# Two decoder blocks in one kernel: ACT builds the compressed blocks, the last gates move beside the embedding, the rotation angles follow the norm

## The reference, cut to what matters

```python
# first block, layer i
def compress(kv, pe, w1, w2):            # 31 overlapping blocks of 32 tokens, stride 16
    blocks = kv[:, :, idx, :] + pe       # pe: position inside the block
    return jax.nn.silu(blocks.reshape(B, G, NC, 32 * dh) @ w1) @ w2
...
h = h + concatenate([y_hg, y_nsa]) @ w_out[i]
gate = jax.nn.sigmoid(rmsnorm(h, ple_norm_g[i]) @ w_pg[i])
h = h + gate * (p[i] @ w_pp[i])          # p[i] @ w_pp[i]: the embedding
...
# second block, layer 0
x = layer_norm(a * x + 0.5 * swiglu_ffn(x, ...))
h = diff_attention(x, ..., cos(positions * inv), sin(positions * inv), ...)
```

## Time and profile before

| | us |
|---|---|
| Three timed runs: median (lowest to highest) | 3279.15 (3272.29 to 3296.4) |
| The profiled execution: its own time | 3269.5 |
| Its span, first to last instruction | 3267.7 |
| PE busy | 3063.7 (94%) |
| POOL, DVE, ACT busy | 1363.3, 1165.8, 1100.6 |
| Granted clock of PE, mean over the span | 0.968 |

### The profile page before, as it was taken

The page is one execution under the profiler, slowest core; times in us unless marked ns, Lnnn a source line. Parts: engine busy times, 40 slices in busy tenths (PEclk is TensorE's granted clock), DMA queues, the critical chain, the costliest instruction groups (busy, mean ns, idle before and its releaser), DMA issues.

```text
span 3267.7 us, 58661 instructions
## 1 busy us (share of the span) xinstructions
PE 3063.7 (94%) x24228; PEld 2806.5 (86%) x24228; DVE 1165.8 (36%) x1930; ACT 1100.6 (34%) x1823; POOL 1363.3 (42%) x656
## 2 busy tenths in 40 slices
PE   7999898999899999989889999999999978999998
PEld 7987488987578999979469789998999967789997
DVE  1535742444743111152751541103211085441103
ACT  4233633223633222131634342223222133432222
POOL 5533044443133454444026255444445444254543
PEclk9999999999999999999989999999999998999999
DMA  5211013212012223222013222232233231122231
GB/s 190 71 55 62 1 65 115 73 46 72 14 52 73 96 96 103 90 76 86 19 64 109 69 81 96 96 103 78 92 101 101 96 112 62 55 84 96 96 103 58
DMA packets 72202, 262.22 MB, mean 80 GB/s; under 512 B 8032, under 2 KB 8672, under 8 KB 70912
## 3 DMA queue, kind: packets, MB, share of 16 engines
q1 hardware_dynamic: 69728, 249.77, 23.2%
q10 hardware_dynamic: 2336, 10.49, 0.9%
HBM read 258.13 MB, written 2.10 MB: 80 GB/s over the span
## 4 chain that ended last, share of the span: by engine, by line
PE 81%; DVE 11%; issue 4%; ACT 2%; POOL 2%; DMA 0%; POOLq 0%; ACTq 0%; DVEq 0%
PE bank L527 24%; PE bank L509 15%; PE bank L511 15%; PE bank L513 15%; PE bank L668 1%; PE bank L841 1%; PE bank L873 1%; PE bank L857 1%; POOL wl L381 1%; PE bank L1080 1%; DVE small L2086 1%; DVE s L1673 1%; PE bank L719 1%; PE bank L1071 1%; DVE h L1968 1%
## 5 line engine op out<-in xcount | busy, mean ns | idle before, releaser
L381 POOL TENSOR_TENSOR wl<-raw,wh 128x1024 fp32r<-128x1024 f32 x464 | 1154.2, 2502 | 1815.8 <-ACT wh L1147 1815.6
L1147 ACT CAST wh<-raw 128x1024 fp32r<-128x1024 f32 x464 | 472.1, 1047 | 1053.9 <-PE bank L513 837.6
L509 PE MATMUL bank<-xh,wh 128*128 128x256 f32 x3168 | 641.1, 284 | 0.0
L511 PE MATMUL bank<-xl,wh 128*128 128x256 f32 x3168 | 625.1, 279 | 0.0
L513 PE MATMUL bank<-xh,wl 128*128 128x256 f32 x3168 | 624.5, 279 | 0.0
L509 PEld LDWEIGHTS bank<-xh,wh 128*128 128x128 f32 x3168 | 485.0, 190 | 19.7 <-issue 18.3
L513 PEld LDWEIGHTS bank<-xh,wl 128*128 128x128 f32 x3168 | 484.1, 190 | 0.0
L511 PEld LDWEIGHTS bank<-xl,wh 128*128 128x128 f32 x3168 | 484.0, 190 | 0.0
L527 PE MATMUL bank<-xh,wh 128*128 128x256 f32 x1952 | 392.5, 283 | 54.1 <-ACT xh L1199 36.6
L527 PE MATMUL bank<-xh,wl 128*128 128x256 f32 x1952 | 390.1, 282 | 0.0
L527 PEld LDWEIGHTS bank<-xh,wh 128*128 128x128 f32 x1952 | 304.2, 194 | 65.2 <-issue 64.5
(11 more groups left out here) (336 smaller groups left out, 3816.6 us busy)
## 6 DMA issues: line engine op xcount, KB each, us to landing
raw<-in_slabs SPq DMA_DIRECT2D x464, 512.0 KB, 3.3
h<-in_x_t SPq DMA_DIRECT2D x8, 256.0 KB, 5.3
w1v<-in_w ACTq DMA_DIRECT2D x2, 1024.0 KB, 4.7
side<-in_pp_w ACTq DMA_DIRECT2D x2, 1024.0 KB, 5.3
xm<-in_mem_t ACTq DMA_DIRECT2D x2, 1024.0 KB, 4.8
out<-h SPq DMA_DIRECT2D x8, 256.0 KB, 2.0
side<-in_w SPq DMA_DIRECT2D x1, 1024.0 KB, 12.6
vt<-in_p_t ACTq DMA_DIRECT2D x2, 512.0 KB, 6.2
```

Of the source, the lines that this page charges most:

```text
L381: nc.gpsimd.tensor_tensor(wl[:, n % RING, :], raw[:, n % RING, :], wh[:, n % RING, :], A.subtract).then_inc(w_low, 1)
L509: nc.tensor.matmul(dst[:, c], high_l, high_r[:, c], start=first and n == 0, stop=False)
L511: nc.tensor.matmul(dst[:, c], high_l, low_r[:, c], start=False, stop=False)
L1147: nc.scalar.copy(wh[:, slot, :], raw[:, slot, :]).then_inc(w_high, 1)
```

## The change

Three edits, which share no code:

1. *Compressed blocks.* `placed` moves from POOL to ACT. Where POOL made eight positions at once (two instructions of 128x496 for each tensor), ACT makes one position with each instruction, 16 of 128x62 for each tensor, as an Identity activation with the embedding's column as bias. ACT copies `kk_k` one chunk earlier.
2. *Last gates.* A new semaphore, `gates`, is raised when the fourth pair's product is done, ahead of its embedding; ACT's last sigmoids wait for it. DVE waits for the embedding itself. In layer 1, squares and sums of squares are left out (no norm reads them), `split` copies each chunk as soon as it is final, the two weight slabs that `pg` cast are cast inside `split` behind the sixth copy, and DVE makes six of the eight lower halves ahead of the last gates.
3. *Angles.* The three DMAs of `da_prep` are issued in the norm before it, between ACT's wait for the first statistic and the square of the mean. DVE goes on to `da_prep` when `h` is written, without waiting for POOL's `xl`. The clamp of `r` (input of the first sine) is put ahead of the two steps that make `r2`.

```diff
-    "front": dict(... kk=8, blocks=4, ...),
+    "front": dict(... kk=8, blocks=32, ...),
...
 # POOL, front
                     low(chunk0 + 11 + lv)
-                    if lv == 4:
-                        placed(0, kk_k, blocks_k)
-                    if lv == 5:
-                        placed(1, kk_v, blocks_v)
...
 # PE, hidden
-                        pe.wait_ge(S["blocks"], st["blocks"] + 2 * b + 2)
+                        pe.wait_ge(S["blocks"], st["blocks"] + 16 * b + 16)
...
 # PE, pg
                     last = pair(st["slab"] + 2 * j, j % 2, xh, xl, T, *two_steps)
+                    if j == 3:
+                        last.then_inc(S["gates"], 1)
...
 # ACT, norm
                 act.wait_ge(S["stat"], st["stat"] + 1)
+                if (st["kind"], st["layer"], st["which"]) == ("ln", 0, 0):
+                    act.dma_start(dpos[:], positions.broadcast_to([P, T])).then_inc(block2_in, 16)
+                    act.dma_start(dspr[:], spread).then_inc(block2_in, 16)
+                    act.dma_start(rot_m, rot2).then_inc(block2_in, 16)
...
 # ACT, split of layer 1
-                    act.wait_ge(S["r"], st["r"])
-                    split_of(st, lambda c: h[:, c, :])
+                    for c in range(KC):
+                        act.wait_ge(S["r"], st["r"] - KC + c + 1)
+                        nc.scalar.copy(xh[:, c, :], h[:, c, :]).then_inc(S["xh"], 1)
+                        if c == KC - 3:
+                            high(st["slab"] - 2 + RING)
+                            high(st["slab"] - 1 + RING)
...
 # ACT, front
+                def placed(b, kk, x):
+                    act.wait_ge(S["kk"], st["kk"] + 4 * b + 4)
+                    tok = kk.rearrange("p g (c i r) -> p i g c r", i=8, r=2)[:, :, :, :, 0]
+                    for i in range(16):
+                        nc.scalar.activation(x[:, i, :].rearrange("p (g c) -> p g c", g=2),
+                                             tok[:, i % 8, :, i // 8:i // 8 + NC], F.Identity,
+                                             bias=par(COL1, "pe", (st["layer"] * 2 + b) * 16 + i)).then_inc(S["blocks"], 1)
...
 # ACT, pg
+                    else:
+                        act.wait_ge(S["gates"], st["gates"] + 1)
...
 # DVE, norm
-                if unsplit:
+                if unsplit or (ln and (st["layer"], st["which"]) == (0, 0)):
                     dve.wait_ge(S["hn"], st["hn"] + KC)
...
 # DVE, pg
                     dve.wait_ge(took_a, st["took"] + j + 1)
+                    if j == 3:
+                        if st["layer"]:
+                            for c in range(KC - 2):
+                                lower(st, c, h[:, c, :])
+                        dve.wait_ge(prod, st["prod"] + 4)
...
 # DVE, da_prep
                 step(V.tensor_scalar(r2, r, float(np.pi / 2), None, A.add))
+                V.tensor_scalar(r, r, PI, -PI, A.min, A.max).then_inc(S["dp_v"], 1)
                 step(V.tensor_scalar(k, r2, float(np.pi), None, A.is_gt))
```

More of the change, by code:

```diff
@@ L84 @@
     "split": dict(xh=KC, xl=KC),
-    "front": dict(slab=36, prod=36, took=2, ev_a=ACT_TOOK[-1], ev_v=DVE_TOOK[-1], kk=8, blocks=4, cmp_p=5, cmp_a=5,
+    "front": dict(slab=36, prod=36, took=2, ev_a=ACT_TOOK[-1], ev_v=DVE_TOOK[-1], kk=8, blocks=32, cmp_p=5, cmp_a=5,
                   cmp_v=3, lvl_k=4 * (LEVELS - 2), lvl_v=4 * LEVELS, lvl_p=4 * LEVELS, lbs=2, ax=12, hpv=4, ob=4,
@@ L90 @@
     "w_out": dict(slab=8, prod=4, took=4, r=KC // 2, sq=KC // 2, s2=KC - 2, s1=1, e2=1),
-    "pg": dict(slab=8, prod=4, took=4, r=KC, sq=KC, s2=KC - 2),
+    "pg": dict(slab=8, prod=4, took=4, gates=1, r=KC, sq=KC, s2=KC - 2),
     "ffn_in": dict(slab=2 * NF, prod=NF, took=NF, hh=NF, hv=NF, hl=NF),
@@ L130, in plan @@
             add["xh"] = add["xl"] = KC
+        if kind == "pg" and layer == 1:
+            add["sq"] = add["s2"] = 0
         if kind == "w_out" and which == 0:
@@ L424, in decayed @@
                         nc.gpsimd.tensor_tensor(k, k, cat(odd, k.shape[2]), A.mult).then_inc(S["lvl_k"], 1)
[L426 to L434, removed]
                 def cosine(j):
@@ L1289, in head_out @@
                     nc.scalar.copy(ob[:, hd, :], bank[hd][:]).then_inc(S["ob"], 1)
-                for j in range(11):
+                for j in range(10):
                     chunk(j)
@@ L1294, in front @@
                 pairs_of(kk_k, proj[:, KCM, :])
+                chunk(10)
+                placed(0, kk_k, blocks_k)
                 chunk(11)
@@ L1297, in front @@
                 pairs_of(kk_v, proj[:, VCM, :])
-                for j in range(12, 14):
-                    chunk(j)
+                chunk(12)
+                placed(1, kk_v, blocks_v)
+                chunk(13)
                 table(F.Silu)
@@ L1463, in pg @@
                     nc.scalar.activation(sg[:, 1, :], bank[2 * (j % 2) + 1][:], F.Sigmoid).then_inc(took_a, 1)
-                    if j == 3:
-                        table(F.Abs_reciprocal_sqrt)
-                        high(st["slab"] + 2 * j + RING)
-                    squares(st, 2 * j)
-                    squares(st, 2 * j + 1)
-                high(st["slab"] + 7 + RING)
+                    if st["layer"] == 0:
+                        if j == 3:
+                            table(F.Abs_reciprocal_sqrt)
+                            high(st["slab"] + 2 * j + RING)
+                        squares(st, 2 * j)
+                        squares(st, 2 * j + 1)
                 if st["layer"] == 0:
+                    high(st["slab"] + 7 + RING)
                     act.dma_start(side[:], w1[1, 0]).then_inc(w1k_in, 16)
@@ L1736, in split @@
             def split(st):
-                for c in range(KC):
+                for c in range(KC - 2 if st["which"] == 1 else 0, KC):
                     lower(st, c, (proj[:, (HGO if c < 4 else NZ - 4) + c, :], h[:, c, :], xq[:, c, :])[st["which"]])
@@ L2014, in pg @@
                         V.tensor_tensor(h[:, c, :], h[:, c, :], tb[:, o, :], A.add).then_inc(S["r"], 1)
+                    if st["layer"]:
+                        dve.wait_ge(S["r"], st["r"] + 2 * j + 2)
+                        continue
                     for o in range(2):
```

10 lines of the change are left out of this document (4 added, 6 removed).

## The result

| | median | runs |
|---|---|---|
| before | 3282.0 us | 14 (3269.4 to 3310.4) |
| changed | 3259.8 us | 14 (3247.2 to 3277.2) |

The ratio is 0.994, with a 95% interval of 0.9919 to 0.9961: 20 us less (13 to 27; the medians differ by 22). It lies beside the forecast's 3263 and its -15.7 us. The profiled executions are only 10.1 us apart (span 3267.7 and 3257.6), less than the change's own places give; that difference is the first thing to explain.

What follows compares the result with a forecast made beforehand. PE was taken as the bound, 81% of the chain. Terms -15.1 - 0.25 + 0.1 - 0.45 = -15.7 us on the profiled 3269.5, carried in proportion to the median 3279.15, gave 3263 us; range 3251 to 3279.

Steps and rivals of the forecast that it cites:

- Term A: Front, recurrence steps of both layers: moving the blocks' positions off POOL removes most of four PE waits; -15.1 us, bounds -16 and -6.
- Rival 1: Front: POOL's `hk` multiplies follow `wl` and hold DVE instead; 8.4 us stay, gain 8.3, about 3271 us; chance 12%.
- Nothing for ACT: Front: both sets of 16 activations fit into ACT's idle time, so no cost was taken for ACT.
- 16 are 3.5 us: Front, ACT: one set of 16 activations, sized from a 0.22 us activation of the same width, takes 3.5 us.
- activations of `blocks` at about 0.2 us: Front, ACT: sign that the forecast is right, each activation for the positions lasting about 0.2 us.
- the cover ends at (9.1 - 1.6) / 16 = 0.47 us each: Front, ACT: values' activations stay hidden up to 0.47 us each, since `hidden()` reads them 9.1 us after the product.
- Rival 3: `hidden()`, both layers: PE waits for ACT's second set; 3285 us in all at 1.05 us per activation; chance 3%.
- Term B0: Layer 0's last gates: sigmoids start earlier, but POOL's `wl` holds DVE's adds; -0.25 us, bounds 0 and -1.3.
- Term B1: Layer 1's last gates and split: POOL's `wl` holds DVE's sixth lower half; +0.1 us, bounds +0.5 and -1.9.
- Rival 4: Layer 1's last gates: gates early, but PE starts no earlier because `took_v` is late; inside the forecast, no separate chance.
- Term C: Rotation angles: operand earlier by 1.0 and 0.15, less 0.7 for the DMA issues; -0.45 us, bounds +0.7 and -4.5.
- So I take no gain: First rotation, L975: PE might keep its clock after a shorter wait of about 2.5 us; counted as 0.

## Why the prediction was right, step by step

- **Term A, -15.1: right, -15.2 measured** in the windows, -15.6 in the sections, -15.1 between whole kernels. The residue taken from the level before was right too (0.15 to 0.2 us for each place; the step of 2.40). Rival 1's mechanism is real and its price was too high: POOL's `hk` follows `wl` at once and holds DVE's second multiply, but only for 0.48 us of 0.66, and PE doesn't stand. The working has two slips that move nothing: the four stands are 10.2 us, not 10.4, and by its own figures rival 1 gains 16.4 - 8.4 = 8.0 us, not 8.3.
- **Nothing for ACT: right in the sum, wrong in two of its steps.** "16 are 3.5 us" was mis-sized, and so was the sign "activations of `blocks` at about 0.2 us": 4.80, a third more. Of the 1.3 us too little, 0.9 is the stride (3.90 from consecutive words) and 0.4 is there without it. And "the cover ends at (9.1 - 1.6) / 16 = 0.47 us each" came near the measured 0.50 for the wrong reason: it looked at who reads the blocks, while the first to suffer is POOL's `hk`, queued behind a `wl` that waits for ACT's cast. Rival 3 was real, its place was not, and its price was too low: at 0.73 us each its formula gives 16 x 0.73 - 7.5 + 1.6 = 5.8 us a layer, the run paid 10.
- **Term B0, -0.25: the hold was right** (2.18 us for the two adds), the start came 0.34 earlier. The further 0.8 us of the two executions shown is not the change's. From the embedding's first matmul (3464) to number 3564 it is 28.8, 27.2 and 27.2 us in three executions with the old gates, 26.9 in four with the new ones and 28.4 in the run with consecutive words, without the slower pace: 0.34 less, and 1.6 more when the clock falls otherwise.
- **Term B1, +0.1: the mechanism was right** to 0.02 us (POOL first by 0.15, forecast 0.13; the sixth half held), the size was short: "L2009 and L2010 end at 1030.57, and PE starts at 1030.7" left 0.1 us for what took 0.55 (L2025's end at 1019.25 to PE's start at 1019.80). +0.47 in seven executions with six halves ahead. Two hundred matmuls behind the embedding's start (6936 to 7136) nothing of it can be seen: 34.0 to 34.6 us in three executions with the old order, 33.8 to 34.8 in the seven. Rival 4, that PE does not start earlier for `took_v`, describes it.
- **Term C, -0.45: the DMA issues right** (+0.7, measured 0.73, and gone when moved); the cast's end earlier by 1.4, with those 0.7 taken out, instead of 1.0. From the second statistic to a point behind the first rotations (matmuls 10120 to 10300), without the slower pace, 37.4, 35.7 and 35.7 us in three executions with the old code and 35.4, 35.2, 35.2 and 33.4 in four with the new: -1.5 on average, with up to 2.0 between executions of one code. "So I take no gain" for the clock was the step that was too careful, and the before trace's wait of 3.65 was the longer one of 3.65, 3.0 and 3.0 in three executions with the old code.
- **Sum**: -15.7 forecast, -17.8 by places in the two executions shown (-17 with B0 at -0.34), -15 between whole kernels without the slower pace, -20 (13 to 27) timed. Carrying the profiled difference over to the median was sound, but the prediction took the runs' scatter, 7 us, as mere noise around one time. In the profiled executions most of it is the slower pace, in steps of 14 us; that this holds for the runs without a profile is likely, not shown. Terms B0, B1 and C are each smaller than the scatter: that the sum came within 5 us of the timed difference supports Term A and says nothing of them, and only the windows do.

## What to carry to other kernels

Before an activity is moved to an idle engine, ask which of that engine's next instructions another engine waits for, and what stands behind that wait in its order: here the blocks had time, the `hk` multiplies two queues further did not. Before filling a wait with work, look at what releases the engine that stands: DVE's six halves were useful work, and four of them stood ahead of the one instruction that PE needed; two fill the gap just as well, for 6.7 us. When two single executions differ by less than the scatter of the runs, lay them side by side matmul by matmul: the places that change and the places that only differ come apart at once.

## What the runs showed that was not expected

- PE has two paces at the full granted clock, 113.3 and 117.8 ns from one 128x256 matmul to the next, for whole stretches or loops. Some stretches have the same in all thirteen profiled executions (matmuls 40 to 180 always the slower, 300 to 660 always the faster), others change from one execution to the next. A loop of 3100 matmuls costs 14 us more at the slower. Over the executions the total was 12 to 58 us, which is as large as the scatter of the timed runs (41 us over the 14 of before). The cause is open.
- ACT's 62-wide activation from SBUF with a bias per partition lasts 0.387 us and steps by 0.294 at a stride of 64 bytes, 0.332 and 0.238 from consecutive words.
- A cast of 128x512 from int32 with its one input in SBUF took 1.37 us beside POOL's subtraction instead of 0.43, so it is held too, with one input. The same section of the Trainium skill names casts among what can contend, in the modes that use both ports. The trace agrees in that the cast was held; in which mode it ran, no row shows.
